# Two attentions of a four-layer block: value products with the transposed probabilities stationary

## The reference

```
def attend_blocks(q, k, v, scale):
    def one(qi):
        s = jnp.einsum('bqhgd,bkhd->bhgqk', qi, k).astype(jnp.float32) * scale
        p = jax.nn.softmax(s, axis=-1).astype(v.dtype)
        return jnp.einsum('bhgqk,bkhd->bqhgd', p, v)
    o = lax.map(one, qb)

def even_layer(...):
    oa = neighbourhood_attention(qa, ka, va, rpb)
    ob = attend_blocks(qb, kb, vb, D_HEAD ** -0.5)
    o = jnp.concatenate([oa.reshape(B, S, -1), ob.reshape(B, S, -1)], -1) * jax.nn.silu(gate)
    return o @ w_out

def odd_layer(...):
    oc = attend_blocks(qc, kc, v_c, (C_NOPE + C_ROPE) ** -0.5)
    od = diff_attend_blocks(qd[:, :, :, 0], qd[:, :, :, 1], kd[:, :, :, 0], kd[:, :, :, 1], vd, lam, D_HEAD ** -0.5)
    od = rmsnorm_2(od, g_sub_d) * (1.0 - lam_init)
    o = jnp.concatenate([oc.reshape(B, S, -1), od.reshape(B, S, -1)], -1) * jax.nn.silu(gate)
    return o @ w_out
```

## Time and profile before

| | us |
|---|---|
| median of three runs | 2983.1 (2982.58 to 2985.28) |
| the profiled execution | 2981.21 |
| its span, from the first to the last instruction | 2979.5 |
| axial attention, from its first score product to the first turn of the output stage | 1799.0 to 1996.9 |
| latent attention, the same | 2642.1 to 2875.3 |

### The profile page before, as it was taken

The page is one execution under the profiler, slowest core; times in us unless marked ns, Lnnn a source line. Parts: engine busy times, 40 slices in busy tenths (PEclk is TensorE's granted clock), DMA queues, the critical chain, the costliest instruction groups (busy, mean ns, idle before and its releaser), DMA issues.

```text
span 2979.5 us, 42870 instructions
## 1 busy us (share of the span) xinstructions
PE 2835.1 (95%) x15248; PEld 2386.9 (80%) x15248; DVE 1768.1 (59%) x3125; ACT 1175.9 (39%) x2142; POOL 1341.3 (45%) x962
## 2 busy tenths in 40 slices
PE   7999998999999999999999999999999978889999
PEld 6688957777888878888888788987888776678877
DVE  3799937438666651313057578971224839978861
ACT  3311166334222221313123457761323536767750
POOL 2233124464777776663255334335341534333235
PEclk9999997899999999999999999999999989999999
DMA  4123243332222126443865442405426753131223
GB/s 139 68 96 137 71 106 75 114 127 78 85 85 80 48 83 207 127 141 123 150 203 181 127 113 66 118 22 172 151 85 227 223 153 71 49 79 36 84 85 128
DMA packets 224370, 336.30 MB, mean 113 GB/s; under 512 B 81910, under 2 KB 152438, under 8 KB 223686
## 3 DMA queue, kind: packets, MB, share of 16 engines
q1 hardware_dynamic: 200790, 289.88, 32.5%
q10 hardware_dynamic: 22192, 39.98, 3.7%
q0 software_dynamic: 1216, 4.20, 0.5%
HBM read 235.20 MB, written 98.81 MB: 112 GB/s over the span
## 4 chain that ended last, share of the span: by engine, by line
PE 84%; DVE 6%; issue 3%; ACT 3%; DMA 2%; POOL 1%; SPq 1%; DVEq 0%; POOLq 0%; ACTq 0%; PEldq 0%
PE psum L737 16%; PE psum L2937 14%; PE psum L2569 8%; PE psum L3288 8%; PE psum L444 7%; PE psum L1275 4%; PE psum L1306 4%; PE psum L1286 4%; PE psum L530 3%; PE psum L1573 2%; PE psum L984 2%; PE psum L962 1%; PE psum L973 1%; PE psum L3597 1%; PE psum L2243 1%
## 5 line engine op out<-in xcount | busy, mean ns | idle before, releaser
L737 PE MATMUL psum<-parts_even,parts_ffn 128*128 128x512 f32 (+1 forms) x1344 | 287.4, 375 | 0.0
L2937 PE MATMUL psum<-parts_ffn 128*128 128x512 f32 x1152 | 273.9, 392 | 3.2 <-issue 2.3
L737 PE MATMUL psum<-parts_odd 128*128 128x496 f32 (+1 forms) x1344 | 270.0, 361 | 6.2 <-POOL parts_odd L652 5.4
L737 PEld LDWEIGHTS psum<-parts_even,parts_ffn 128*128 128x128 f32 x1344 | 238.5, 188 | 44.5
L737 PEld LDWEIGHTS psum<-parts_odd 128*128 128x128 f32 x1344 | 227.4, 191 | 42.0 <-POOL parts_odd L652 5.6
L2937 PEld LDWEIGHTS psum<-parts_ffn 128*128 128x128 f32 x1152 | 217.1, 189 | 50.8 <-issue 2.5
L444 PE MATMUL psum<-parts_mixer 128*128 128x512 f32 x912 | 210.0, 391 | 0.3 <-DVE parts_mixer L287 0.3
L444 PEld LDWEIGHTS psum<-parts_mixer 128*128 128x128 f32 x912 | 170.4, 188 | 35.8 <-DVE parts_mixer L287 0.5
L2311 DVE TENSOR_SCALAR_CACHE_REDUCE choose_flags<-arena,choose_bits 128x384 uint8<-128x384 f32 (+2 forms) x198 | 174.3, 942 | 1.2
L3288 PE MATMUL psum<-parts_ffn 128*128 128x512 f32 x720 | 167.3, 389 | 2.9 <-DVE arena L3094 1.6
L2937 PE MATMUL psum<-up_t,parts_ffn 128*128 128x512 f32 x684 | 168.7, 394 | 0.0
(11 more groups left out here) (423 smaller groups left out, 6501.3 us busy)
## 6 DMA issues: line engine op xcount, KB each, us to landing
arena<-ffn_down_k SPq DMA_DIRECT2D x44, 512.0 KB, 3.7
arena<-x SPq DMA_DIRECT2D x8, 2048.0 KB, 9.2
x<-arena SPq DMA_DIRECT2D x24, 512.0 KB, 4.0
arena<-w_in_e SPq DMA_DIRECT2D x24, 512.0 KB, 4.6
e_tokens<-arena ACTq DMA_DIRECT2D x24, 512.0 KB, 3.2
arena<-w_in_o SPq DMA_DIRECT2D x24, 496.0 KB, 6.0
arena<-ffn_up_b SPq DMA_DIRECT2D x11, 1024.0 KB, 4.8
up_raw_two<-ffn_up_b SPq DMA_DIRECT2D x11, 1024.0 KB, 4.9
```

The costliest lines, as they stand in the source:

```text
L737: last = pe.matmul(self.bank(t, n), self.hT[:, a, k, t * P:(t + 1) * P], w, start=(k, a, b) == (0, 0, 0), stop=(k, a) == (KT - 1, 1))
L2937: last = pe.matmul(self.core.psum[:, bank, :], slot[:, a, k, :], operand[b][:, k, :], start=opens and (k, a, b) == (0, 0, 0), stop=(k, a) ...
```

## The change

In both attentions the value product changes sides. The stationary operand is now 128 keys by 128 queries of the transposed probabilities, and the values stream: 128 columns (high and low values) against the high probabilities, 64 columns (high values only) against the low ones. So a tile takes sixteen products, eight of each width, into one bank (6 or 7 by turns) and comes out with the queries on the partitions, the high half in columns 0 to 63 and the low half beside it. The turn back is gone, and so are the pair grouping and the folded identity. ScalarE now takes the first half times the inverse sum to SBUF (`halve`), and VectorE adds the second half times the inverse sum (`finish`). The gate is multiplied by GpSimd, one instruction for each head (`weigh_by_gate`, 128 by 512), and the stage after waits for that. `attend` follows `turn` by one step, and the results follow one step later, where before the last step was the sixth.

```
@@ class WideAttention, gpsimd
-        with pool.Fori(0, rounds - 1) as i:
+        def weigh_by_gate(i, s):
+            pool.wait_ge(self.finished, N * i + N // 2 * (s + 1) + self.SLOTS)
+            here = self.out_sb[:, :, self.heads[s](i, self.dv)]
+            pool.tensor_tensor(here, here, self.gate[:, :, self.heads[s](i, self.dv)], ALU.mult).then_inc(self.gated, 1)
+
+        hold(pool, self.gate_ready)
+        with pool.Fori(0, self.rounds - 1) as i:
             for s in range(2):
                 pool.wait_ge(self.scored, N * i + N // 2 * (s + 1))
                 self.part_scores(pool, i + 1, s)
...
                 self.part_values(pool, i + 1, s)
-                store(i, s)
-        if self.ahead is not None:
-            self.ahead(pool)
+                weigh_by_gate(i, s)
         for s in range(2):
-            store(rounds - 1, s)
+            weigh_by_gate(self.rounds - 1, s)
@@ tensor
-                for b in range(4 * h, 4 * h + 4):
-                    if self.doubled:
-                        pairs = [(self.vp[:, s, b], 0), (self.vp[:, s, b], 1)]
...
-                    for m, (values, part) in enumerate(pairs):
-                        last = pe.matmul(ps[:, 6, 0:2 * P], values, self.pT[:, g % 2, part, b], start=(b, m) == (0, 0),
-                                         stop=(b, m) == (KT - 1, len(pairs) - 1))
...
-                    last = pe.matmul(ps[:, 7, j * self.dv:(j + 1) * self.dv], self.oT[:, here], self.fold, start=True, stop=True)
...
+        def attend(i, n):
...
+            pe.wait_ge(self.finished, N * i + n + self.SLOTS - 1)
+            for b in range(KT):
+                if b % 4 == 0:
+                    pe.wait_ge(self.low_out, 2 * N * i + 2 * n + b // 4 + 3)
+                products = [(0, 2 * dv), (1, dv)]
+                for m, (part, columns) in enumerate(products if b < KT - 1 else products[::-1]):
+                    last = pe.matmul(ps[:, 6 + n % 2, 0:columns], self.pT[:, n % self.SLOTS, part, b], self.vp[:, s, b, 0:columns],
+                                     start=(b, m) == (0, 0), stop=(b, m) == (KT - 1, 1))
+            last.then_inc(self.attended, 1)
@@ scalar
-            act.activation(self.oT, ps[:, 6, 0:2 * P], ACT.Copy).then_inc(self.taken, 1)
+        def halve(i, n):
+            act.wait_ge(self.attended, N * i + n + self.SLOTS + 1)
...
+            act.activation(self.high_half[:, n % 2], ps[:, 6 + n % 2, 0:dv], ACT.Copy, scale=self.inv[:, n % 4:n % 4 + 1]).then_inc(self.halved, 1)
@@ vector
-                for j in range(2):
-                    last = dve.scalar_tensor_tensor(out=self.out_sb[:, t + j, columns], in0=ps[:, 7, j * dv:(j + 1) * dv],
-                                                    scalar=self.inv[:, n % 4 + j:n % 4 + j + 1], in1=self.gate[:, t + j, columns],
-                                                    op0=ALU.mult, op1=ALU.mult)
+            dve.wait_ge(self.halved, N * i + n + 1)
+            dve.scalar_tensor_tensor(out=self.out_sb[:, t, self.heads[s](i, dv)], in0=ps[:, 6 + n % 2, dv:2 * dv], scalar=self.inv[:, n % 4:n % 4 + 1],
+                                     in1=self.high_half[:, n % 2], op0=ALU.mult, op1=ALU.add).then_inc(self.finished, 1)
@@ class GatedBranches, turn
-        if n == 3:
+        if n in (2, 3):
+            hold(pe, [(finished, count + n - 3) for finished, count in self.second_out])
+        if n == 8:
             hold(pe, self.second_done)
```

More of the change, by code:

```diff
@@ L1128, in __init__ @@
             self.heads.append(at_head)
[L1129 to L1138, removed]
+        self.results_out = [(self.finished, self.SLOTS + self.N * self.rounds)]
+        self.done = [(self.gated, 2 * self.rounds)]
         self.exps_done = [(self.expd, 2 + self.N * self.rounds)]
-        self.results_out = [(self.finished, 2 + self.G * self.rounds)]
     @staticmethod
     def shared_place(region):
-        return region.take(2, 2, KT * 2 * P, dtype=F32R).rearrange("p a b (k t) -> p a b k t", t=2 * P), region.take(2, S)
+        return region.take(8 * S, dtype=F32R), region.take(2, S)
     def run(self, engine, order, aside=None):
@@ L1312, in back @@
-        def back(i, n):
-            if n % 2:
-                return
-            g = n // 2
-            if g == 0:
-                pe.wait_ge(self.folded, 1)
-            pe.wait_ge(self.taken, G * i + g + 2)
-            pe.wait_ge(self.finished, G * i + g + 2)
-            for j in range(2):
-                here = slice(j * P, (j + 1) * P)
-                if self.doubled:
-                    last = pe.matmul(ps[:, 7, j * self.dv:(j + 1) * self.dv], self.oT[:, here], self.fold, start=True, stop=True)
-                else:
-                    last = pe.transpose(ps[:, 7, here], self.oT[:, here], self.core.ident)
-            last.then_inc(self.backed, 1)
@@ L1328, in tensor @@
-        self.run(pe, lambda step: (step(scores, 0), step(turn, -2), step(attend(0), -4), step(attend(1), -5), step(back, -6)))
+        def attend(i, n):
+            s = n // TT
+            if n % TT == 0:
+                pe.wait_ge(self.parted[s], 6 * i + 7)
+            pe.wait_ge(self.finished, N * i + n + self.SLOTS - 1)
[7 more added lines that the diff above has]
+            last.then_inc(self.attended, 1)
@@ L1330, in scalar @@
+        self.run(pe, lambda step: (step(scores, 0), step(turn, -2), step(attend, -3)))
     def scalar(self, act):
-        N, G, ps = self.N, self.G, self.core.psum
+        N, ps, dv = self.N, self.core.psum, self.dv
         hold(act, self.act_after)
-        act.sem_inc(self.taken, 1)
         def exps(i, n):
@@ L1401, in finish @@
         def finish(i, n):
[L1402 to L1404 removed]
             s, t = divmod(n, TT)
[L1406 to L1427 removed]
+            dve.wait_ge(self.halved, N * i + n + 1)
+            dve.scalar_tensor_tensor(out=self.out_sb[:, t, self.heads[s](i, dv)], in0=ps[:, 6 + n % 2, dv:2 * dv], scalar=self.inv[:, n % 4:n % 4 + 1],
+                                     in1=self.high_half[:, n % 2], op0=ALU.mult, op1=ALU.add).then_inc(self.finished, 1)
+        self.run(dve, lambda step: (step(finish, -4), step(peak, 0), step(low, -2), step(inverse, -3)), self.vector_aside)
 class DiffAttention:
@@ L4809, in build @@
                                  prep.done + rest.taken_out + gone.done,
-                                 scales.done + prep.done + rest.weights.raw_free() + st.multiplied + gone.done, own, there, shared))
+                                 prep.done + rest.weights.raw_free() + st.multiplied + gone.done, own, there, shared))
         diff_rows, diff_gate, latent_rows = (block4(place + 4 * S * n) for n in range(3))
```

117 lines of the change are left out of this document (28 added, 89 removed).

## The result

The changed kernel takes 3085.5 us (median of 5 runs, 3076.7 to 3087.4) against 2982.6 us for the kernel before (5 runs, 2973.1 to 2985.3). The ratio is 1.035, with a 95% interval of 1.033 to 1.037. The forecast was 3072 us, with a range of 3033 to 3110. The profiled span grew from 2979.5 to 3084.5 us, by 105.0.

What follows compares the result with a forecast made beforehand. TensorE was taken to bound both attention loops, with GpSimd's in-order queue late at the ends. Loops 55, ends 30 and clock 4 summed to +89 us on 2981.2, giving a forecast of 3072 us, range 3033 to 3110.

Steps and rivals of the forecast that it cites:

- Columns or loads: Value products in both loops: weight loads, not columns, set a 106 ns distance; loops +55 us (32 to 88) after waits.
- The waits that went: TensorE's present waits, 5 to 6 us in the latent loop and about 2 in the tails, disappear: 7 us off.
- The ends: After E, the last value product's end, GpSimd's queued gates and slices delay output products: +14.7 even, +15.3 odd, together +30 us.
- The clock: At both ends TensorE mostly stands still, so its clock falls and restarts slowly: +4 us (0 to 8).
- A: Value products in the loops: load and stream overlap better, 81 ns apart; loops +10 us, total 3027 us; chance 0.08.
- B: Loops: fp32r loads hide fully, only columns count, VectorE becomes the bound; 2988 us, no real change; chance 0.07.
- C: Loops as B, with VectorE packing without gaps, and the ends at their lower bound with warm clock; 2963 us; chance 0.03.
- D: TensorE's clock falls inside a loop and stays down; one attention at half clock costs +224 us, 3296 us; chance 0.05.

Runs made afterwards that it cites:

- x2: The changed kernel, with the product of the low probabilities streaming 128 columns instead of 64; 3082.0 us, ratio 1.0345.
- x3: The changed kernel, with the high product streaming 64 columns instead of 128 in six of eight key blocks; 3083.0 us, ratio 1.0335.
- x8: The kernel before, with each 256-column value product split into two of 128, values still stationary; 3078.8 us, ratio 1.0375.
- x4: The changed kernel without the low-probability product in six of eight key blocks, so ten products a tile; 3043.9 us, ratio 1.0204.
- x7: The kernel before, gates on GpSimd (last ones behind the third weight slice), turn back by two transposes, halves added as in the change; 2987.7 us, 1.0017.
- x9: x7 with `halve` last in ScalarE's step and `finish` behind the subtraction in VectorE's; 3017.5 us, ratio 1.0132.
- x1: The changed kernel, with GpSimd's last two `weigh_by_gate` of each attention moved behind the third weight slice; 3048.7 us, ratio 1.0237.

## Why the prediction was right

**Columns or loads.** The prediction took the load to set the distance, because plain float32 products of 64 columns were stretched without a reason in their stream. That the columns do not set it and the number of products with their loads does held, and x2, x3 and x8 show it from three sides. The step that was off is the size of that term: 106 ns were taken, from plain float32, and 113 to 114 came. That makes the tile 1.81 us instead of 1.70, and 128 x (1.81 - 1.215) = +76, less some 5 for waits that went away: +70.6 where +55 was forecast, within its bounds of 32 and 88. The range held this because the upper bound had been taken from the 256-column distance. A better row stood in the same trace: in the mixer's L2044, plain float32 products of 97 columns with 128x128 operands, 144 instructions take 16.22 us, which is (16.22 - 0.275) / 143 = 0.1115 us apart. The distance of 120 ns at 256 columns, which is that of the right format, also pointed above 106.

**The waits that went.** TensorE's waits for the subtraction in the latent loop, 6.2 us before, are 2.8 us in the changed kernel:

```profile
PE psum L1264 <- DVE both L1334: 2.8, 4, 0.7
```

All idle time of TensorE between the first score product and E fell from 3.5 to 2.5 us in the axial loop and from 7.9 to 4.1 in the latent one. I had taken off 7 for all waits; 4.8 can be read here. (The "5 to 6 us over the stage" was itself low: 1.44 of 50 us over 231.5 is 6.7.) VectorE's share was forecast at 0.8 and is 0.77 and 0.74; the steps at 3.5 and 3.9 us and are 3.58 and 4.03.

**The ends.** Even: forecast +14.7, measured +14.4. The gate begins at E + 0.74 (0.75), the third output product at E + 22.0 (22.3). Odd: forecast +15.3, measured +17.5. There the gate begins at E + 1.65 instead of 0.75, because VectorE has two normalising instructions of 1.22 us in its stream ahead of the last `finish`:

```profile
2959.93 1.22 DVE L4283 TENSOR_TENSOR arena<-arena 128x1024 f32<-128x1024 f32 x1
2961.19 1.22 DVE L4284 TENSOR_TENSOR arena<-arena 128x1024 f32<-128x1024 f32 x1
2962.34 0.47 DVE L1348 SCALAR_TENSOR_TENSOR arena<-psum,latent_raw,latent_raw 128x64 f32<-128x64 f32 x2
```

The prediction had looked for what is queued behind the new wait, not for what stands before the instruction that it waits for.

**The clock.** Forecast +4. At the even end it cost nothing: the third slice was done at 2057.29 us and its product began at 2057.44, so GpSimd still set the pace. In the odd layer the first output product took 2.91 us instead of 1.65, which is 1.3 us on the path. So the term was +1.3, not 4; the 0.9 us above make up the rest of that end.

**Sum.** 55 + 30 + 4 = 89 was forecast; 70.6 + 31.9 = 102.5 came, and 2.5 us ahead of the attentions, where both kernels have the same code. As to the rivals: A (81 ns), B and C (columns) are excluded by the distance and by x2. D did not come in the changed kernel. The Trainium skill's 81 ns a product at 128 columns ("TensorE: Matmul & The Clock Gate", section "Back-to-back issue gap") does not hold for the fp32r products here: in x8 all sixteen stream 128 columns, and they lie 114 ns apart.

## What to carry over

Swapping the two sides of a product is to be priced by the number of products, each with its load, first and by columns second: up to 128 columns (here 113 ns, against 120 at 256 columns), a narrower stream gives nothing back. When an operation moves to an engine that has room, find what is queued behind its last instance: here sixteen short instructions cost nothing inside the loops, but the last two of each attention cost 32 us at the two ends, and all of it came back by moving them behind work that does not wait for the attention. And the tenth that the next engine has free is no measure of the gain to be had: chains between engines with in-order streams ended x4, x7 and x9 before any engine was full.

## What the runs showed of the hardware

- fp32r products with a 128x128 stationary operand lie 113 to 115 ns apart at 64 and at 128 columns, with either operand stationary, in groups of sixteen and of ten.
- A busy share of 100% on TensorE in the profile does not say that it is the bound. PE read 50.00 of 50 us in x4, where the loop was held by a chain of waits; its load share, 0.85 against 0.94, told the two apart.
- The clock falls after the stalls: 0.50 at the even end, where TensorE was busy 4.46 of 14 us, and 1.00 again in the stretch from 2056 on, where it was busy throughout. It falls inside a loop too. In x4 it was 0.58 over 20 us, after a stretch with 3.6 us of waits in 20. In x7 the waits before a fall were shorter: 1.10 and 1.67 us, the second ending at 2702.4, and the value product behind it took 2.06 us instead of 1.20.
- Stages whose code is the same differ between executions. The first axial score product came at 1799.1 us before, at 1801.6 in the changed kernel and at 1789.7 in x1. In x1 the difference arises in the causal attention, whose first score product comes at 454.2 us before and 458.5 in x1, and the output stage behind it at 564.8 and 555.5. The changed kernel's 3 us arise ahead of it, since it is already at 457.2 there. Before and x1, in the same window:

```profile
505.00:555.00 50.00, 43.44 (x264) 39.88 (x263) 38.94 (x80) 27.72 (x67) 14.60 (x9) 0.77 0.07 17
```
```profile
505.00:555.00 50.00, 42.58 (x309) 38.77 (x307) 39.22 (x85) 28.91 (x70) 19.59 (x12) 0.90 0.12 33
```

The granted clock is 0.77 in the one and 0.90 in the other. Such a difference of up to 12 us is 0.4% of the time, and the code ahead of the attentions is the same in both, so none of it belongs to the change. Between the two attentions x1 is 6 us slower than the kernel before (644.6 against 638.6). It is why the parts above are read between points of one trace and not from its total.
